# A buffer of lower halves placed 32 bytes past a multiple of 64 bytes

## What is computed

```python
u = rms_norm(h, norm_mix[i])
z, xbc, dt_raw, q_a, c_kv, k_rope, gate_ssd, gate_mla = split_cols(u @ w_in[i], IN_SPLITS)
...
u = rmsnorm(h, attn_pre_norm[i])
proj = u @ w_in[i]
...
u = rmsnorm(h, ffn_pre_norm[i])
gate, up = jnp.split(u @ w_gate_up[i], [D_FF], axis=-1)
y = (jax.nn.silu(gate) * up) @ w_down[i]
h = h + rmsnorm(y, ffn_post_norm[i])
h = h + (p[i] @ ple_proj[i]) * jax.nn.sigmoid(h @ ple_gate[i])
```

## Time and profile before

| what | us |
|---|---|
| median of 3 runs | 1050.97 |
| lowest, highest | 1047.4, 1055.92 |
| span of the profiled execution | 1050.0 |
| PE busy in it | 994.2 |
| DVE busy | 626.8 |
| ACT busy | 514.3 |

### The profile page before, as it was taken

One profiled execution on the slowest core, in us unless ns is written; L12 is line 12 of the kernel. 1 busy time (PEld: TensorE's weight loads), 2 busy tenths in 40 slices (PEclk: granted clock), 3 DMA queues, 4 the chain that ended last, 5 costly groups with the idle time before them and its releaser, 6 DMA issues.

```text
span 1050.0 us, 19418 instructions
## 1 busy us (share of the span) xinstructions
PE 994.2 (95%) x8568; PEld 919.7 (88%) x8568; DVE 626.8 (60%) x833; ACT 514.3 (49%) x693; POOL 19.7 (2%) x23
## 2 busy tenths in 40 slices
PE   7999999999999999999996587799999999999998
PEld 6999999899989999997673455499999999999998
DVE  6798789868766875443110110189985755555566
ACT  5576497844675563523110111277666653443453
POOL 0000021001000000000000000000000000000000
PEclk9999999999999999999998988899999999999999
DMA  7665453446245357888999999954323356555531
GB/s 290 246 236 192 170 201 124 168 156 236 81 150 212 139 224 297 315 354 333 420 420 420 421 419 423 394 192 177 139 81 128 119 206 205 196 181 189 193 121 41
DMA packets 34871, 241.74 MB, mean 230 GB/s; under 512 B 4064, under 2 KB 4448, under 8 KB 6368
## 3 DMA queue, kind: packets, MB, share of 16 engines
q1 hardware_dynamic: 33264, 233.32, 58.3%
q0 software_dynamic: 1232, 6.99, 1.9%
q10 hardware_dynamic: 288, 0.15, 0.1%
HBM read 239.36 MB, written 1.08 MB: 229 GB/s over the span
## 4 chain that ended last, share of the span: by engine, by line
PE 76%; DMA 12%; DVE 7%; ACT 2%; SPq 2%; issue 1%; DVEq 0%; ACTq 0%
PE ps L479 18%; PE ps L481 18%; PE ps L480 18%; DMA wr<-in_c_weights 8%; PE ps L568 3%; PE ps L1278 3%; DMA T8b<-in_c_weights 3%; SPq L3053 2%; DVE wlo L2044 2%; PE ps L965 1%; PE ps L1228 1%; DVE xs L2276 1%; ACT whi L1388 1%; PE ps L1305 1%; PE ps L830 1%
## 5 line engine op out<-in xcount | busy, mean ns | idle before, releaser
L2044 DVE TENSOR_TENSOR wlo<-raw,whi 128x2048 fp32r<-128x2048 f32 (+1 forms) x119 | 271.2, 2282 | 113.7 <-ACT whi L1388 113.3
L479 PE MATMUL ps<-XUh,whi 128*128 128x256 f32 x992 | 280.4, 283 | 0.7 <-DVE wlo L2044 0.6
L480 PE MATMUL ps<-XUl,whi 128*128 128x256 f32 x992 | 276.2, 278 | 0.0
L481 PE MATMUL ps<-XUh,wlo 128*128 128x256 f32 x992 | 276.2, 278 | 0.0
L1388 ACT ACTIVATE whi<-raw 128x2048 fp32r<-128x2048 f32 (+1 forms) x119 | 225.0, 1893 | 47.7 <-PE ps L481 41.2
L479 PEld LDWEIGHTS ps<-XUh,whi 128*128 128x128 f32 x992 | 186.5, 188 | 2.7 <-issue 1.7
L480 PEld LDWEIGHTS ps<-XUl,whi 128*128 128x128 f32 x992 | 188.0, 189 | 0.7 <-issue 0.5
L481 PEld LDWEIGHTS ps<-XUh,wlo 128*128 128x128 f32 x992 | 186.2, 188 | 0.0
L2976 DVE SCALAR_TENSOR_TENSOR sphs<-sphs,wsl,ps 128x256 f32<-128x256 f32 x8 | 3.8, 480 | 91.0 <-ACT sphs L2009 71.8
L479 PE MATMUL ps<-ffnah,whi 128*128 128x256 f32 x176 | 49.5, 281 | 0.0
L480 PE MATMUL ps<-ffnal,whi 128*128 128x256 f32 x176 | 49.5, 281 | 0.0
(11 more groups left out here) (624 smaller groups left out, 2372.9 us busy)
## 6 DMA issues: line engine op xcount, KB each, us to landing
raw<-in_c_weights SPq DMA_DIRECT2D x137, 1024.0 KB, 4.9
wr<-in_c_weights SPq DMA_DIRECT2D x36, 1024.0 KB, 26.1
xhi<-in_c_weights SPq DMA_DIRECT2D x12, 1024.0 KB, 26.3
xlo<-in_c_weights SPq DMA_DIRECT2D x12, 1024.0 KB, 26.5
extra<-in_c_weights SPq DMA_DIRECT2D x10, 1024.0 KB, 27.5
T<-in_c_weights SPq DMA_DIRECT2D x5, 1024.0 KB, 26.1
T8b<-in_c_weights SPq DMA_DIRECT2D x5, 1024.0 KB, 26.4
acb<-sums POOLq DMA_DIRECT2D x4, 1024.0 KB, 4.9
```

Source lines behind the costliest of these rows:

```text
L479: pe.matmul(ps, h(k), xh(k), start=start and k == 0, stop=False, skip_group_check=loose)
L480: pe.matmul(ps, h(k), xl(k), start=False, stop=False, skip_group_check=loose)
L481: t = pe.matmul(ps, l(k), xh(k), start=False, stop=stop and k == kt - 1, skip_group_check=loose)
L2044: dve.tensor_tensor(l[:, 0:n], r, h[:, 0:n].bitcast(F32), ALU.subtract).then_inc(*did("w_lo", "split", i))
```

## The change

```diff
     xu_at = at[0]
-    XUh, XUl = sb("XUh", [128, 8, 256], F32R), sb("XUl", [128, 8, 256], F32R)
+    XUh = sb("XUh", [128, 8, 256], F32R)
+    XUl = sb("XUl", [128, 8, 256], F32R, at[0] + 32)
+    at[0] += 8 * KB + 64
     H = sb("H", [128, 8, 256], F32)
```

## The result

The changed kernel takes 1070.73 us (median of 6 runs, 1070.17 to 1072.6) against 1049.83 us for the kernel before on the same chip (6 runs, 1046.63 to 1055.92): 1.021 times the time, with a 95% interval of 1.0185 to 1.0236. The profiled executions differ by as much, with spans of 1070.8 and 1050.0 us. The change costs 2%, some 21 us.

The account below looks back on a forecast made before the run. The prediction took PE, busy 95% of the span with a stream of `triple`s, to bound the kernel. Its four terms, 0 + 0 + 0 + 0, left the forecast at about 1051 us, with a range of 1040 to 1072 us.

Parts of the forecast that it names:

- fetched twice: Rival at line 480: reads of `XUl` that straddle blocks are fetched twice, wholly or partly, up to 102 us; chance 0.26.
- no change: Likeliest case, the forecast itself: 1051 us for the kernel, 1046 to 1056 us with the pitch states; chance 0.46.
- step (2): `H`, `T8`, `T8b`, constants and the region move by 64 bytes; claimed 0 us for DMA and for PE.
- step (3): PE reads `XUl` as moving operand 992 times at 32 past a multiple of 64; claimed 0 us, upper bound 102 us.
- Step (1): VectorE writes `XUl` at its new place in 16 instructions; claimed 0 us.
- The router's row: 32 router matmuls at starts 0, 16, 32 and 48 past 64, median 279 ns; taken as showing no odd-start cost.
- One more block: Rival: each long read of `XUl` at line 480 fetches one further block, 7.0 us, giving 1058 us; chance 0.14.
- Step (4): PE loads `XUl` as stationary operand 64 times in the exchanged products; claimed 0 us, upper bound 6.6 us.
- The two pitches: Dense streams on PE run at 113.3 or 117.8 ns a matmul, a state taken at a stream's start and kept.
- all to the higher, 12.4 us more: Bound if all 2,750 matmuls at the lower pitch went to the higher, 4.5 ns each.
- `ffnal` and `XVl` keep theirs: Sign for reads fetched twice: these operands keep their durations while the triple grows to up to 443 ns.
- A part without `XUl` (the experts' part) changes by more than 2 us: Sign that the forecast is wrong: the part at 475 to 680 us changes length, speaking against 0 us for the region.

Follow-up runs that it names:

- e4_all_at_0: Kernel before with 64 bytes left free ahead of `XUh`, so all moving operands start at the weights' place modulo 256; 1073.18 us against 1048.01, ratio 1.0236.
- e2_only_region: Kernel before with `XUl` left in place and only the buffers behind it moved on by 64 bytes; 1057.6 us against 1046.66, ratio 1.0102.
- e5_dma_256: Kernel before with `raw`, `whi`, `wlo` and `extra` moved to multiples of 256, moving operands still 192 from the weights; 1044.04 us against 1047.4, ratio 0.9961.
- the micro kernels: Three kernels computing nothing of the reference, only streams of 48 fp32r matmuls with moving operands and weights at chosen starts; pitches 113.3 to 123.5 ns.

## Why the prediction failed where it did

The range of 1040 to 1072 us held the 1070.7 us, by luck: its upper edge came from cutting the chance of reads that are fetched twice, which isn't what happened. The value is off: *no change*, 1051 us, was the likeliest case, and "within 1%" had the largest chance. What came was slower by 2%, the side that had 0.28. Two terms of the sum failed: the 0 us for the region as PE reads it, in step (2), and the 0 us for `XUl` as moving operand, in step (3).

**What bounds the kernel: right. That a slower matmul goes into the time one to one: right in the dense stretches, too much for the whole.** PE was idle neither before nor after in the dense stretches. Over the whole kernel about four fifths of what the streams gained or lost arrived in the span: 17.7 of 20.8 us outside the experts' part here, 19.9 of 24.4 us in `e4_all_at_0`.

**Step (1), VectorE, 0 us: right.** Busy for 626.9 us against 626.8: writing `XUl` 32 bytes off cost it nothing.

**Step (2), the region moves by 64 bytes, 0 us: wrong for PE.** In the streams it cost 10.5 us (9.0 in the region's, 1.1 in `ffna`, 0.4 in the exchanged chunks with `MM`), and alone 1.02% of the time (`e2_only_region`). The sentence that failed is "for PE, operands of both kinds run at both pitches: `XUl` and `XUh` at 113 and 118 ns". Both of these started 64 past a multiple of 128. There was no row in the trace with a moving operand at a multiple of 128 and the weights at one, so rows 4 and 5 said nothing about it. One place of the trace of before hinted that starts might matter, and the prediction doesn't use it: in the exchanged products, where the distance is 64 and not 192, the pitch was 117.8 ns in all eight chunks of this trace and never 113.3 (the earlier trace rows have 280 ns for them and 278 for the normal ones). It looked like the higher pitch; as one number for a whole class of streams it deserved a question. The DMA side of the step was right: `wr` still lands 26.1 us after its issue and `T8b` 26.5 instead of 26.4. But the earlier trace rows compared 64 past a multiple of 128 with 128 past a multiple of 256, and so had no buffer at a multiple of 256, the start that `e5_dma_256` showed to be quicker.

**Step (3), `XUl` as moving operand, 0 us: wrong, by +10.3 us.** The router's row was the wrong neighbour. Its matmuls move 36 columns, and a matmul that short doesn't show what the long reads cost; they are plain fp32 besides, 16 matmuls in 32 records. It excluded, as the text says, "a cost per start, not one per block of a long read", and then I gave it the greater weight all the same. But neither rival had the mechanism. *One more block* had 7.1 ns for each line 480, and *fetched twice* up to 102.7 ns (a bound misread besides: the 216 ns of the earlier trace rows are one of the two records of a plain fp32 matmul, and the 32 records are 16 matmuls of 432 ns); the micro kernels have streams with every moving operand off 64 at 113.3 ns. The term is 3.4 ns a matmul as a mean over the triple, and not on line 480 (482 after) alone: over all `XU` streams the steps behind the three matmuls went from 115.5, 115.6 and 115.3 ns to 119.2, 122.1 and 115.4. So a matmul that reads `XUh` at its old place pays more than half as much as the one that reads `XUl`, and the other one nothing. A stream with operands at 192 and 224 has a pitch of its own (119.0 ns behind all five lead-ins, with the same three steps). So the 7.0 us of the *one more block* rival are near the 10.3 us of this term by accident, and its place is wrong.

**Step (4), `XUl` as stationary operand, 0: right.** The four chunks with `XU` stationary have 117.7 ns before and after; the 0.4 us of the exchanged chunks are in the four with `MM` stationary, whose place moved with the region (117.8 to 119.9 ns), and belong to step (2).

**The two pitches: half right.** That streams of the same tiles run at 113.3 or 117.8 ns and keep the one they begin with is so, and the micro kernels reproduce it. That it has nothing to do with addresses ("a difference without any change of address") was true of those two rows and misleading as a picture: it made the pitch look like a matter of luck, when the pair of starts decides which pitches there are to choose from. The bound of that part, "all to the higher, 12.4 us more", was thus none: the streams went beyond the higher pitch, to 118.9 and 120.0 ns.

**The signs named in advance.** "Line 480 should keep 276 to 281 ns": 283. "The forecast is wrong if line 480 differs from line 481 in pitch by more than about 4 ns": by the steps behind them, 122.1 against 115.4 ns, it does, where before it was 115.6 against 115.3. "`ffnal` and `XVl` keep theirs" if reads were fetched twice: they did not, which is what turned the search to step (2). "A part without `XUl` (the experts' part) changes by more than 2 us": it did, by 3.1 us, but this sign was badly chosen. In `e2_only_region`, with the same places for all of its buffers, the same part is as long as before. The stretch from its first to its last instructions in the kernel before and in `e2_only_region`:

```profile
466.90:687.40 220.50, 181.83 (x1844) 127.98 (x1844) 41.25 (x115) 40.67 (x99) 1.06 (x2) 0.92 0.97 401
```

```profile
474.40:695.00 220.60, 181.77 (x1845) 127.14 (x1845) 41.28 (x115) 40.76 (x99) 1.06 (x2) 0.92 0.97 400
```

Both have the clock at 0.92 and 400 GB/s, where after has 0.90 and 395 GB/s. So those 3 us aren't the shift. The profiled execution of the changed kernel is the slowest of its six (1072.6 us, the others 1070.17 to 1071.61). What lowered the rate in it stays open.

**What stays open.** Why the pair of starts sets the pitch. The Trainium skill, *TensorE: Matmul & The Clock Gate*, in its steps of a matmul, gives the engine two independent read ports for SBUF, one for the moving operand and one for the weights. By that the place of the one against the other would cost nothing, and here it costs up to 120.0 - 113.3 = 6.7 ns a matmul. That the two reads meet somewhere is a guess; no run here tests it. The Trainium skill's *SBUF — State Buffer*, cited ahead for its lines of 16 bytes, doesn't account for this either: starts that are all multiples of 16 differ by those 6.7 ns. A start of 4 is slower still (123.4 ns); no run here tells whether lines of 16 bytes have to do with it.

## What to carry to other kernels

In a stream of dense matmuls, the start of the moving operand relative to the weights' start is a parameter of the layout, worth up to 6% of the stream here, and 2% of this kernel when it went from a mixture of 113.3 and 117.8 ns to 119 and 120 ns (the way back, to 113.3 ns in nearly all streams, showed no gain of its own in the medians): before a buffer is moved, list every buffer that the address cursor moves along with it, and read the pitch (distance between starts) of each stream at its old and new place, since durations and busy shares hardly show it. Round addresses are no safe choice: both operands at the same place modulo 256 gave 120.0 ns every time that they lay on multiples of 64. And where a row of the trace is to exclude a cost, it has to have the same size and the same pair of places as what is changed, or it only bounds; a pitch that looks random in the trace can still depend on what is about to be changed.

## What the runs showed of the chip that was not expected

- A stream of 128x256 fp32r matmuls with changing weights has a small set of stable pitches at full clock, from 113.3 to 120.0 ns for starts at multiples of 16 with the weights at a multiple of 256; the pair of starts modulo 256 sets which, and at 64 and 192 a stream takes 113.3 or 117.8 ns at its start and keeps it.
- The weights' own start matters too: of the starts tried, the one that gave 113.3 ns in every stream is 208 with the weights at 16, 144 with them at 32 and 112 with them at 0; at 48 none did.
- A moving operand in a mixed triple sets the pitch of its neighbours: `xh` at 192 with `xl` at 224 gave 119.0 ns behind all five lead-ins, with unequal steps of 119, 122 and 115 to 116 ns, while 192 alone gave 113.3 or 117.8 and 224 alone 118.3.
- In the DMA-bound part, 1 MB pieces (128 partitions of 8 KB) land 2.43 to 2.44 us apart when their destination starts at a multiple of 256, 2.48 to 2.49 us apart when it is 64, 112, 128 or 192 past one, and 2.50 us apart when it is 16 past one (medians for `raw`, `xhi`, `xlo` and `wr` in the kernels above): some 2% of the rate for the start of a destination.
